# Merge, projection and feed-forward stages share a block; last chunks run tile by tile

## The chip, the cores and the metric

The kernel runs on one core of a Trainium2 chip. The core has a matrix engine (PE), a vector engine (DVE), a scalar engine (ACT), a general engine (POOL) and a queue engine (SP) that only issues DMAs here. The metric is the device time of one execution in microseconds, lower is better.

## What is computed

Two transformer stacks of two layers each, in float32, on 512 tokens with 1024 features. The part of a layer that the change touches reads, for the first stack:

```
x = x + (g_a * o_a + g_b * o_b + g_c * o_c) @ w_out
h = rms_norm(x, g_ffn)
x = x + jnp.square(jax.nn.relu(h @ w_ff1)) @ w_ff2
```

and for the second stack (two branches, six modulation vectors from `c @ mod_w[l] + mod_b[l]`):

```
x = x + g1 * _mixer(h, positions, w_in[l], forget_bias[l], w_branch_a[l], w_branch_b[l], w_out[l])
h = _rmsnorm(x, norm2_g[l]) * (1.0 + sc2) + sh2
x = x + g2 * _conv_ffn(h, w_up[l], conv_w[l], conv_b[l], w_down[l])
...
    u = conv_b + sum(conv_w[i] * up[:, i:i + S] for i in range(CONV_W))
    a, b = jnp.split(u, 2, axis=-1)
    return (jax.nn.silu(a) * b) @ w_down
```

## The kernel before

Activations are kept transposed: a tile is 128 features by 512 tokens, and x has eight (k = 0 to 7). A product runs in split precision: `moving_hi` (a_hi) is the rounded tile and `moving_lo` (a_lo) the rest, and the weights have the same two parts. A chunk is one slab of weights, 128 by 1024, and yields one PSUM bank in most stages: eight tiles k, each three matmuls (high by high, high by low, low by high), 24 matmuls of 128x512. SP loads slabs into a ring of four. For each chunk ACT makes the high weights (L208), POOL subtracts to get the low weights (L234), both into two buffers that alternate. ACT also makes the high part of a tile (L250 or L2295) and DVE the low part (L255 or L2320).

The stages of a layer in question, in order, are:

- `merge_stage`: each branch's output times its projection, gated on DVE (L1178, L1211, L1213) and added to `scratch` (L1188, L1218). 12 chunks of half height in the first stack, 8 in the second; its last chunk fills two banks, output tiles 6 and 7. In the second stack DVE also multiplies modulation weights (L2490), and PE sums them over partitions with one-column matmuls (L2451, `over_partitions`).
- `linear_stage` ("projection", wout): eight chunks, one bank each. DVE adds the bank to x (L2365, or L2909 in the second stack), ACT squares it (L540), DVE adds up the squares (L548).
- First stack, `squared_up_stage` ("up"): 32 chunks. PE sums the squares over partitions (L2276), ACT and DVE make the reciprocal root (L2297 to L2326), PE spreads it (L2281). Each bank is evacuated by DVE with relu and that root (L2331) and squared on ACT (L2307).
- Second stack: a `norm_stage` (not touched), then `gated_up_stage`: 44 chunks, ACT copies each bank (L2828), DVE does the three taps of the convolution and the gate (L2866 to L2879, L2857), ACT the sigmoid (L2821).
- `down_stage`: contracts the hidden tiles, two per block, into all eight banks (L648, at the end L634).

Each stage opens a block of its own. All engines end it together: each drains, they meet at a barrier (L117), POOL clears the semaphores of the block before, and all start the next. Inside a stage, semaphores order the work. A stage's first two chunks are interleaved in `first_products` (L312): for each tile k as soon as it is split, high and low weights of chunk 0 on its high part, then chunk 1, then the low parts. `keep_busy` (L290) issues matmuls on a constant whose result nobody reads, at the ends of stages.

A matmul on full float32 data (one column, 128 columns, or L290's) is one row of the instruction order but two records in the trace.

## Time and profile before

| | us |
|---|---|
| three timed runs | 3581.09, 3584.23, 3584.91; median 3584.23 |
| profiled execution, whole | 3583.43 |
| its span | 3581.7 |
| PE busy in it | 3437.8 (96%) |
| DVE, POOL, ACT busy | 2015.3, 1586.3, 1436.2 |
| mean granted clock of PE | 0.981 of full speed |

In the timeline rows below, the first number is the start of an instruction (or of several merged ones, "x8") in microseconds from the start of the span, the second its duration. Matmuls are pipelined: eight of them in a row last 1.98 us, but the next starts 1.82 us after the first. What stands in brackets is the idle time of the engine before the row and what ended it.

### The profile page before, as it was taken

What the parts mean: (1) busy time and instruction counts of PE and PEld (TensorE: products, weight loads), DVE (VectorE), ACT (ScalarE), POOL (GpSimd) and SP (SyncE); (2) the same over time, 40 slices, a digit from 0 to 9 for tenths busy, and PEclk for the clock granted to TensorE, in tenths of its full rate; (3) what the DMA queues carried; (4) which work ended last, traced back from release to release, by engine and by line L of the source; (5) the groups of instructions that cost most, each with busy time, mean ns of one, the idle gap of its engine ahead of it and who ended that gap; (6) DMA issues with size and microseconds to landing.
All of it is one profiled execution on the core that took longest, in us unless ns stands there. A gap on an engine that the chain in (4) does not pass through costs nothing. (4 is left out here: it accounts for less than half of the span.)

```text
span 3581.7 us, 44753 instructions
## 1 busy us (share of the span) xinstructions
PE 3437.8 (96%) x15838; PEld 2818.8 (79%) x15838; DVE 2015.3 (56%) x3260; ACT 1436.2 (40%) x2516; POOL 1586.3 (44%) x827
## 2 busy tenths in 40 slices
PE   7999999999999999999999999999999999999998
PEld 6877787788888777878887877778877877778877
DVE  5775655112367756641224666658964666658953
ACT  3256743232333567332323446233333446333332
POOL 3346453444444563534443641335543641335543
PEclk9999999999999999999999999999999999999999
DMA  4311123222232111322343221432343221432322
GB/s 165 103 57 37 36 89 106 93 94 95 88 124 97 45 42 46 114 83 94 106 146 108 72 89 60 165 112 103 131 153 107 72 89 56 164 112 104 134 89 94
DMA packets 96746, 346.62 MB, mean 97 GB/s; under 512 B 12624, under 2 KB 13264, under 8 KB 95952
## 3 DMA queue, kind: packets, MB, share of 16 engines
q1 hardware_dynamic: 96592, 344.62, 27.9%
q8 instruction: 91, 1.49, 0.2%
q14 instruction: 63, 0.52, 0.0%
HBM read 338.15 MB, written 6.29 MB: 96 GB/s over the span
## 5 line engine op out<-in xcount | busy, mean ns | idle before, releaser
L234 POOL TENSOR_TENSOR weights_lo<-arena,weights_hi 128x1024 fp32r<-128x1024 f32 x467 | 1189.8, 2548 | 1616.9 <-ACT weights_hi L208 1468.4
L208 ACT ACTIVATE weights_hi<-arena 128x1024 fp32r<-128x1024 f32 x491 | 517.8, 1055 | 622.7 <-PE ps L648 388.1
L302 PE MATMUL ps<-moving_hi,weights_hi 128*128 128x512 f32 x2256 | 568.8, 395 | 11.7 <-ACT weights_hi L208 6.7
L302 PE MATMUL ps<-moving_lo,weights_hi 128*128 128x512 f32 x2256 | 559.5, 390 | 0.0
L302 PE MATMUL ps<-moving_hi,weights_lo 128*128 128x512 f32 x2256 | 557.7, 389 | 0.0
L302 PEld LDWEIGHTS ps<-moving_hi,weights_hi 128*128 128x128 f32 x2256 | 424.1, 189 | 103.3 <-ACT weights_hi L208 7.1
L302 PEld LDWEIGHTS ps<-moving_lo,weights_hi 128*128 128x128 f32 x2256 | 424.1, 189 | 88.3
L302 PEld LDWEIGHTS ps<-moving_hi,weights_lo 128*128 128x128 f32 x2256 | 423.3, 188 | 87.2
L255 DVE TENSOR_TENSOR moving_lo<-arena,moving_hi 128x512 fp32r<-128x512 f32 x196 | 178.0, 959 | 230.9 <-ACT moving_hi L250 230.9
L2331 DVE SCALAR_TENSOR_TENSOR arena<-ps,arena 128x512 f32 x64 | 44.1, 691 | 306.7 <-PE ps L302 292.6
L1015 ACT ACTIVATE arena<-ps,arena 128x512 f32<-128x512 f32 (+1 forms) x320 | 165.9, 525 | 114.8 <-DVE arena L979 114.6
L648 PE MATMUL ps<-moving_hi,weights_hi 128*128 128x512 f32 x800 | 198.1, 390 | 0.0
L648 PE MATMUL ps<-moving_hi,weights_lo 128*128 128x512 f32 x800 | 197.6, 389 | 0.0
L648 PE MATMUL ps<-moving_lo,weights_hi 128*128 128x512 f32 x800 | 197.6, 389 | 0.0
L399 POOL TENSOR_TENSOR weights_lo<-arena,weights_hi 128x512 fp32r<-128x512 f32 x76 | 97.9, 1300 | 197.3 <-ACT weights_hi L208 151.2
L2828 ACT ACTIVATE arena<-ps 128x512 f32<-128x512 f32 x88 | 52.8, 600 | 318.6 <-PE ps L302 302.6
L979 DVE CUSTOM_DVE_ANT_0 ps<-ps,arena 128x512 f32<-128x512 f32 (+1 forms) x320 | 147.1, 519 | 58.8 <-PE ps L927 29.4
L648 PEld LDWEIGHTS ps<-moving_hi,weights_hi 128*128 128x128 f32 x800 | 149.9, 188 | 32.6 <-ACT moving_hi L250 1.6
L648 PEld LDWEIGHTS ps<-moving_hi,weights_lo 128*128 128x128 f32 x800 | 150.2, 188 | 31.2
L648 PEld LDWEIGHTS ps<-moving_lo,weights_hi 128*128 128x128 f32 x800 | 150.2, 188 | 31.1
L948 PE MATMUL ps<-split,split 128*128 128x512 f32 (+3 forms) x640 | 130.1, 333 | 21.8 <-ACT split L1044 19.9
L2876 DVE SCALAR_TENSOR_TENSOR arena<-arena 128x512 f32<-128x512 f32 x88 | 144.5, 1681 | 0.0
(384 smaller groups left out, 5259.6 us busy)
## 6 DMA issues: line engine op xcount, KB each, us to landing
arena<-wstream SPq DMA_DIRECT2D x532, 512.0 KB, 3.3
arena<-modw SPq DMA_DIRECT2D x64, 512.0 KB, 3.7
arena<-modw_first SPq DMA_DIRECT2D x32, 512.0 KB, 4.1
layer_input<-arena SPq DMA_DIRECT2D x2, 2048.0 KB, 6.9
arena<-layer_input SPq DMA_DIRECT2D x2, 2048.0 KB, 8.0
arena<-xT SPq DMA_DIRECT2D x4, 512.0 KB, 5.5
outT<-arena SPq DMA_DIRECT2D x8, 256.0 KB, 2.1
arena<-con SPq DMA_DIRECT2D x1, 1413.5 KB, 9.4
```

The costliest lines, as they stand in the source:

```text
L208: m.nc.scalar.activation(m.w_hi[:, j % 2, :], slab(m, base + at), ACT.Copy).then_inc(hi_ready, 1)
L234: m.nc.gpsimd.tensor_tensor(m.w_lo[:, j % 2, :], slab(m, base + (j if at is None else at)), m.w_hi[:, j % 2, :].bitcast(F32), ALU.subtract)\
L255: return m.nc.vector.tensor_tensor(m.a_lo[:, k, :], tile, m.a_hi[:, k, :].bitcast(F32), ALU.subtract)
L302: mm = m.nc.tensor.matmul(bank, unit_tile(w, k), a[:, k, :], start=(p == 0 and k == 0), stop=(p == 2 and k == KD - 1))
L399: self.m.nc.gpsimd.tensor_tensor(self.m.w_lo[:, j % 2, part], slab(self.m, self.base + j)[:, part], self.m.w_hi[:, j % 2, part].bitcast(F3 ...
L648: mm = nc.tensor.matmul(m.ps[:, 4 * half + n, :], unit_tile(w[:, j % 2, :], 2 * n + k), a[:, 2 * h + k, :], start=(first and p == 0 and k ...
L948: mm = nc.tensor.matmul(m.ps[:, 6, kt * P:T], values(j, b, kt), m.r(part)[:, PT_AT[kt]:PT_AT[kt] + T - kt * P], start=(p == 0 and kt == 0) ...
L979: r = nc.vector.tensor_tensor_reduce(s, s, masks(u // nb, qt), -1.0, HUGE, ALU.add, ALU.min, mx[:, 4 * (u % 2) + qt:4 * (u % 2) + qt + 1])
L1015: a = nc.scalar.activation(prob[:, u % 2, PROB_AT[qt]:PROB_AT[qt] + P * (qt + 1)], m.ps[:, bank, c:c + P * (qt + 1)], ACT.Exp, bias=mx[:, ...
L2331: nc.vector.scalar_tensor_tensor(m.hidden[:, i * BODY + g, :], m.ps[:, g, :], 0.0, rstd, ALU.max, ALU.mult).then_inc(evaced, 1)
L2828: nc.scalar.activation(u[:, s, 2:W], m.ps[:, s, :], ACT.Copy).then_inc(copied, 1)
L2876: nc.vector.scalar_tensor_tensor(acc[:, s, :], u[:, s, 0:T], column(cw, f), acc[:, s, :], ALU.mult, ALU.add).then_inc(tap3, 1)
```

## The change

`chain` opens one block for several stages, and `stage` inside it only adds semaphores. In the first stack merge, projection, up and down of a layer are one chain; in the second stack merge and projection are one, and gated up and down another. A stage now returns an `After`: for the next stage it names the semaphore and count by which a tile of the moving operand has been read (`released`), a tile of the next stage's source is final (`ready`), a bank has been evacuated (`freed`), all weights have been read (`finished`), and functions with the work that the old stage leaves to be put into the next one's program (`act_tail`, `dve_tail`, `pe_tail` and others). The last chunk of a stage runs through `last_products`: for each tile k its three matmuls, then a signal. In merge the last chunk's loops over k and over the three products are swapped. The dummy matmuls between chained stages are dropped. In the second stack the modulation sums of gated up stand before its last four chunks, and those of merge inside the first products of projection. The first turn of the down stage's ACT loop and the last turn of the up stages' loops are written out. `first_layer` wraps merge, `linear_stage(..., leave=True)`, `squared_up_stage` and `down_stage` in one `with chain(m)`.

```diff
@@ -108,21 +109,46 @@
...
 @contextmanager
-def stage(m, names):
-
...
-    ctx = ExitStack()
+def chain(m):
+    ctx, sems = ExitStack(), []
     m.parity = 1 - m.parity
-    sems = [ctx.enter_context(m.nc.semaphore(f"{s}_{m.parity}")) for s in names.split()]
     with m.nc.Block() as block:
...
-        yield block, sems
+        m.chain = block, ctx, sems
+        yield
+    m.chain, m.high_by, m.low_by = None, None, None
     if m.used:
         m.used[0].close()
     m.used = (ctx, sems)
+@contextmanager
+def stage(m, names):
+    with nullcontext() if m.chain else chain(m):
+        block, ctx, sems = m.chain
+        mine = [ctx.enter_context(m.nc.semaphore(f"{s}_{m.parity}_{len(sems)}")) for s in names.split()]
+        sems.extend(mine)
+        yield block, mine
+After = namedtuple("After", "finished released ready freed order total all_ready slots_read act_lead act_tail dve_tail dve_end pe_tail",
...
@@ -303,33 +335,51 @@
...
+    order = after.order or range(KD)
...
+    if after.freed:
+        take(pe, after.freed(0))
+    for n, k in enumerate(order):
+        pe.wait_ge(src_hi, n + 1)
+        product(0, m.w_hi, a_hi, k, start=(n == 0))
...
+    if after.freed:
+        take(pe, after.freed(1))
+    for n, k in enumerate(order):
+        product(1, m.w_hi, a_hi, k, start=(n == 0))
+    if middle:
+        middle(pe)
+    for n, k in enumerate(order):
+        pe.wait_ge(src_lo, n + 1)
+        mm = product(0, m.w_hi, a_lo, k, stop=(n == KD - 1))
     mm.then_inc(chunk_done, 1)
...
+def last_products(pe, m, j, count, bank, hi_ready, lo_ready, released, chunk_done):
+    w_hi, w_lo = m.w_hi[:, j % 2, :], m.w_lo[:, j % 2, :]
+    pe.wait_ge(hi_ready, count)
+    pe.wait_ge(lo_ready, count)
...
+        for p, (w, a) in enumerate(((w_hi, m.a_hi), (w_hi, m.a_lo), (w_lo, m.a_hi))):
+            mm = m.nc.tensor.matmul(bank, unit_tile(w, k), a[:, k, :], start=(k == 0 and p == 0), stop=(k == KD - 1 and p == 2))
+        mm.then_inc(released if k < KD - 1 else chunk_done, 1)
...
@@ -475,104 +525,120 @@
...
+            if leave:
+                if after.freed:
+                    take(pe, after.freed(last))
+                last_products(pe, m, last, body, m.ps[:, last, :], hi_ready, lo_ready, released, chunk_done)
...
+            for k in order:
+                if after.released:
+                    act.wait_ge(*after.released(k))
+                    act.wait_ge(*after.ready(k))
+                split_hi(m, k, source(k)).then_inc(src_hi, 1)
+            for g in range(body):
+                weights_hi(act, m, base, 0, g + 1, body, chunk_done, hi_ready, after=after)
...
+                if g == 0:
+                    act.wait_ge(src_lo, KD)
+                if g < last or not leave:
+                    square(act, g)
...
+            for n in range(2):
+                low(dve, n)
+            if after.dve_tail:
+                after.dve_tail(dve)
+            for n in range(2, KD):
+                low(dve, n)
+            if after.dve_end:
+                after.dve_end(dve)
+            take(dve, after.all_ready)
...
@@ -637,13 +705,13 @@
...
-                    if half == 0 and first and p == 0:
-                        keep_busy(m, 7, 2)
...
                     for n in range(4):
+                        if first and p == 0 and after.freed:
+                            take(pe, after.freed(4 * half + n))
...
@@ -673,19 +741,31 @@
         def _(act):
             def cut(i, h):
                 for k in range(2):
+                    if isinstance(i, int) and i == 0 and after.released:
+                        act.wait_ge(*after.released(2 * h + k))
+                        act.wait_ge(*after.ready(2 * h + k))
                     split_hi(m, 2 * h + k, hidden(i * 4 + 2 * h + k)).then_inc(src_hi, 1)
...
+            if after.act_lead:
+                after.act_lead(act)
+            block_(0, 0, True)
+            block_(0, 1, True)
...
@@ -1099,10 +1182,12 @@
...
-                            for p, (w, a) in enumerate(((m.w_hi, m.a_hi), (m.w_hi, m.a_lo), (m.w_lo, m.a_hi))):
-                                for k in range(4):
+                            for k in range(4):
+                                for p, (w, a) in enumerate(((m.w_hi, m.a_hi), (m.w_hi, m.a_lo), (m.w_lo, m.a_hi))):
                                     mm = nc.tensor.matmul(m.ps[:, 2 * j + n, :], unit_tile(w[:, j % 2, :], 4 * n + k),
                                                           a[:, 4 * (b % 2) + k, :], start=(p == 0 and k == 0), stop=(p == 2 and k == 3))
+                                if n and k < 3:
+                                    mm.then_inc(released, 1)
                             mm.then_inc((first_done, chunk_done)[n], 1)
...
@@ -1132,12 +1217,6 @@
...
-            pe.wait_ge(gated, 8 * (NB - 1) + 2)
-            if not modulate:
-                keep_busy(m, 0, 3)
-            else:
-                pe.wait_ge(mod_added, KD)
-                over_partitions(m, [m.mod_accs[:, q, :] for q in (0, 2)], 0).then_inc(mod_summed, 1)
...
+            last(dve, 6, first_done, 1)
+        def dve_tail(dve):
+            last(dve, 7, chunk_done, 4 * NB + 1)
...
+        def dve_end(dve):
+            dve.wait_ge(mod_summed, 1)
+            for n, part in enumerate((2, 4)):
+                add_modulation_bias(m, part, 1, m.ps[:, 7, KD * n:KD * (n + 1)]).then_inc(mod_biased, 1)
+            dve.wait_ge(mod_biased, 2)
+            modulated_gain(m, 1, 4, "g2")
+        def pe_tail(pe):
+            pe.wait_ge(gated, 8 * NB)
+            pe.wait_ge(mod_added, KD)
+            over_partitions(m, [m.mod_accs[:, q, :] for q in (0, 2)], 7).then_inc(mod_summed, 1)
...
+        return After(finished=(chunk_done, 4 * NB + 1), released=tile_released, ready=lambda k: (added, 8 * (NB - 2) + k + 1),
+                     freed=lambda n: (mod_biased, 2) if modulate and n == 7 else (gated, 8 * (NB - 1) + n + 1),
+                     order=(0, 1, 2, 3, 4, 5, 6, 7) if in_last else (4, 5, 0, 1, 2, 3, 6, 7),
+                     all_ready=(unparked, 16) if parked else None, slots_read=(mod_added, KD) if modulate else None,
+                     dve_tail=dve_tail, dve_end=dve_end if modulate else None, pe_tail=pe_tail if modulate else None)
...
@@ -2263,62 +2364,90 @@
...
-            keep_busy(m, 6, 3)
+            for g in range(BODY - 1):
+                pe.wait_ge(evaced, (iters - 2) * BODY + g + 1)
+                chunk(iters - 1, g)
+            pe.wait_ge(evaced, COUNT - BODY)
+            last_products(pe, m, BODY - 1, COUNT, m.ps[:, BODY - 1, :], hi_ready, lo_ready, released, chunk_done)
...
         def _(act):
+            def high(k):
+                act.wait_ge(*after.released(k))
+                act.wait_ge(*after.ready(k))
+                nc.scalar.activation(m.a_hi[:, k, :], m.x[:, k, :], ACT.Copy, scale=gain(k)).then_inc(src_hi, 1)
             weights_hi(act, m, base, 0, 0, BODY, chunk_done, hi_ready)
-            for k in range(KD):
-                nc.scalar.activation(m.a_hi[:, k, :], m.x[:, k, :], ACT.Copy, scale=gain(k)).then_inc(src_hi, 1)
+            for k in range(KD - 1):
+                high(k)
+            weights_hi(act, m, base, 0, 1, BODY, chunk_done, hi_ready, after=after)
+            after.act_tail(act)
+            high(KD - 1)
             act.wait_ge(summed, 1)
             nc.scalar.activation(root, m.ps[:, SUMS_BANK, 0:TT], ACT.Sqrt, bias=m.eps, scale=1.0 / D).then_inc(rooted, 1)
             nc.scalar.activation(var, m.ps[:, SUMS_BANK, 0:TT], ACT.Identity, bias=m.eps, scale=1.0 / D).then_inc(rooted, 1)
-
...
+            weights_hi(act, m, base, 0, 2, BODY, chunk_done, hi_ready)
+            act.wait_ge(spread_done, 1)
+            nc.scalar.activation(rstd, m.ps[:, SPREAD, :], ACT.Copy).then_inc(spread_out, 1)
...
+            for k in range(KD - 2):
+                low(k)
+            after.dve_tail(dve)
+            low(KD - 2)
+            after.dve_end(dve)
+            low(KD - 1)
...
@@ -2800,13 +2934,27 @@
...
-            with pe.Fori(1, 11) as i:
+            with pe.Fori(1, 10) as i:
...
             pe.wait_ge(mod_added, KD + 1)
             over_partitions(m, [acc_mod], 5).then_inc(mod_summed, 1)
-            keep_busy(m, 6, 4)
+            for s in range(3):
+                pe.wait_ge(copied, 40 + s + 1)
+                split_products(pe, m, base, 10, s, 4, m.ps[:, s, :], hi_ready, lo_ready).then_inc(chunk_done, 1)
+            pe.wait_ge(copied, 44)
+            last_products(pe, m, 3, 44, m.ps[:, 3, :], hi_ready, lo_ready, released, chunk_done)
...
@@ -2925,23 +3088,25 @@
...
+    with chain(m):
+    with chain(m):
+        up = gated_up_stage(m, spare, normed_tiles(m, spare, gain(1), mod(3)))
+        down_stage(m, C2["ff_down"], NF2 // 2, gated_add(5), m.layer + 1 if m.layer + 1 < DEPTH else None, up)
```

How it moves instructions. ACT where projection hands over to up in layer 0 of the first stack; L540 are squares, L208 high weights, L2295 the eight high parts, L2297 and L2298 the root and its argument, L2304 copies the spread root. Before:

```order
L208 ACTIVATE weights_hi<-arena 128x1024
L540 ACTIVATE arena<-arena 128x512
L117 UNCONDITIONAL_BRANCH
L2291 UNCONDITIONAL_BRANCH
L2295 ACTIVATE moving_hi<-arena 128x512 x8
L2297 ACT_TABLE_LOAD
L2297 ACTIVATE arena<-ps,arena 128x4
L2298 ACTIVATE arena<-ps,arena 128x4
L208 ACTIVATE weights_hi<-arena 128x1024
L2304 ACTIVATE arena<-ps 128x512
L2307 ACTIVATE arena<-arena 128x512
L208 ACTIVATE weights_hi<-arena 128x1024
```

After (L238 high weights, L2410 high parts, L570 the square of tile 7, L2419 and L2420 root, L2423 the spread root):

```order
L238 ACTIVATE weights_hi<-arena 128x1024
L2405 UNCONDITIONAL_BRANCH
L2410 ACTIVATE moving_hi<-arena 128x512 x7
L238 ACTIVATE weights_hi<-arena 128x1024
L570 ACTIVATE arena<-arena 128x512
L2410 ACTIVATE moving_hi<-arena 128x512
L2419 ACT_TABLE_LOAD
L2419 ACTIVATE arena<-ps,arena 128x4
L2420 ACTIVATE arena<-ps,arena 128x4
L238 ACTIVATE weights_hi<-arena 128x1024
L2423 ACTIVATE arena<-ps 128x512
L238 ACTIVATE weights_hi<-arena 128x1024
```

The square of tile 7 has moved behind seven high parts and the second chunk's high weights, the eighth high part behind it, and a further chunk's high weights stand before the first square of up.

DVE at the same place; L2365 adds the last bank to x, L548 adds squares, L2320 makes low parts. Before:

```order
L2365 TENSOR_TENSOR arena<-arena,ps 128x512
L548 TENSOR_TENSOR arena<-arena 128x512 x2
L117 UNCONDITIONAL_BRANCH
L2316 UNCONDITIONAL_BRANCH
L2320 SCALAR_TENSOR_TENSOR moving_lo<-arena,moving_hi 128x512 x8
L751 RECIPROCAL arena<-arena 128x4
```

After (L2442 low parts, L2494 the addition to x, L594 the sums of squares):

```order
L2438 UNCONDITIONAL_BRANCH
L2442 SCALAR_TENSOR_TENSOR moving_lo<-arena,moving_hi 128x512 x6
L2494 TENSOR_TENSOR arena<-arena,ps 128x512
L2442 SCALAR_TENSOR_TENSOR moving_lo<-arena,moving_hi 128x512
L594 TENSOR_TENSOR arena<-arena 128x512 x2
L2442 SCALAR_TENSOR_TENSOR moving_lo<-arena,moving_hi 128x512
L835 RECIPROCAL arena<-arena 128x4
```

The evacuation of the last bank has moved behind six low parts.

PE where gated up hands over to down in the second stack; L2451 are the modulation sums, L290 dummies, L648 the first products of down. Before:

```order
L2803 COMPARE_AND_BRANCH
L2451 MATMUL ps<-arena 128x1 x8
L290 MATMUL ps<-arena 128x256 x4
L117 UNCONDITIONAL_BRANCH
L652 UNCONDITIONAL_BRANCH
L290 MATMUL ps<-arena 128x256 x2
L648 MATMUL ps<-moving_hi,weights_hi 128x512 x8
L648 MATMUL ps<-moving_hi,weights_lo 128x512 x8
```

After (L2585 the sums, L334 and L381 gated up's chunks):

```order
L2937 COMPARE_AND_BRANCH
L2585 MATMUL ps<-arena 128x1 x8
L334 MATMUL ps<-moving_hi,weights_hi 128x512 x8
L334 MATMUL ps<-moving_lo,weights_hi 128x512 x8
L334 MATMUL ps<-moving_hi,weights_lo 128x512 x8
...
L381 MATMUL ps<-moving_hi,weights_hi 128x512
L381 MATMUL ps<-moving_lo,weights_hi 128x512
L381 MATMUL ps<-moving_hi,weights_lo 128x512
```

The sums now stand before the last four chunks, the dummies are gone, and the last chunk alternates its three products tile by tile.

## Rows read from the trace of the kernel before

**Rows 1.** The page: busy time by engine; a group with count, busy us, mean ns.

```profile
PE 3437.8 (96%) x15838; PEld 2818.8 (79%) x15838; DVE 2015.3 (56%) x3260; ACT 1436.2 (40%) x2516; POOL 1586.3 (44%) x827
...
L302 PEld LDWEIGHTS ps<-moving_hi,weights_hi 128*128 128x128 f32 x2256 | 424.1, 189 | 103.3 <-ACT weights_hi L208 7.1
```

**Rows 2.** Timeline, handover A: start us, duration, engine, line, operation, [idle before].

```profile
564.44 1.46 PE L290 MATMUL ps<-arena 128*128 128x256 f32 x6
...
579.78 1.98 PE L302 MATMUL ps<-moving_hi,weights_hi 128*128 128x512 f32 x8
```

**Rows 3.** Timeline, handover B, layer 0, PE.

```profile
612.42 1.46 PE L290 MATMUL ps<-arena 128*128 128x256 f32 x6
...
630.22 1.06 PE L2281 MATMUL ps<-arena 128*128 128x128 f32 x8
...
641.80 1.98 PE L302 MATMUL ps<-moving_hi,weights_hi 128*128 128x512 f32 x8
```

**Rows 4.** Timeline, handover C, layer 0, PE.

```profile
797.74 1.98 PE L302 MATMUL ps<-moving_hi,weights_lo 128*128 128x512 f32 x8
...
799.56 1.46 PE L290 MATMUL ps<-arena 128*128 128x256 f32 x6
...
802.90 2.10 PE L648 MATMUL ps<-moving_hi,weights_hi 128*128 128x512 f32 x8
```

**Rows 5.** Timeline, handover D, first layer of the second stack, PE.

```profile
2624.31 1.84 PE L2451 MATMUL ps<-arena 128*128 128x1 f32 x16
...
2626.02 1.97 PE L290 MATMUL ps<-arena 128*128 128x256 f32 x8
...
2632.20 2.12 PE L648 MATMUL ps<-moving_hi,weights_hi 128*128 128x512 f32 x8
```

**Rows 6.** Timeline, handover A2, first layer of the second stack, PE.

```profile
2308.15 1.07 PE L1104 MATMUL ps<-moving_hi,weights_lo 128*128 128x512 f32 x4
...
2330.26 1.98 PE L302 MATMUL ps<-moving_hi,weights_hi 128*128 128x512 f32 x8
```

**Rows 7.** Timeline, handovers A and B of layer 1, PE.

```profile
1529.66 1.46 PE L290 MATMUL ps<-arena 128*128 128x256 f32 x6
...
1545.70 1.98 PE L302 MATMUL ps<-moving_hi,weights_hi 128*128 128x512 f32 x8
...
1578.34 1.46 PE L290 MATMUL ps<-arena 128*128 128x256 f32 x6
...
1609.15 1.98 PE L302 MATMUL ps<-moving_hi,weights_hi 128*128 128x512 f32 x8
```

**Rows 8.** Timeline, last operation of DVE before handover A.

```profile
566.04 0.69 DVE L1218 TENSOR_TENSOR arena<-arena 128x512 f32<-128x512 f32 x1
```

**Rows 9.** Timeline around B: POOL's weights, ACT's high parts, DVE's low parts.

```profile
609.56 2.42 POOL L234 TENSOR_TENSOR weights_lo<-arena,weights_hi 128x1024 fp32r<-128x1024 f32 x1 [3.02 <-ACT weights_hi L208]
...
615.08 5.02 ACT L2295 ACTIVATE moving_hi<-arena 128x512 fp32r<-128x512 f32 x8 [1.11 <-PEq L117]
...
615.84 5.39 DVE L2320 SCALAR_TENSOR_TENSOR moving_lo<-arena,moving_hi 128x512 fp32r<-128x512 f32 x8 [1.13 <-ACT moving_hi L2295]
```

**Rows 10.** Timeline, DVE and POOL at once, after C and at the kernel's start.

```profile
803.88 2.43 POOL L234 TENSOR_TENSOR weights_lo<-arena,weights_hi 128x1024 fp32r<-128x1024 f32 x1 [4.53 <-ACT weights_hi L208]
...
804.35 3.10 DVE L255 TENSOR_TENSOR moving_lo<-arena,moving_hi 128x512 fp32r<-128x512 f32 x2 [0.70 <-ACT moving_hi L250]
...
26.52 4.90 DVE L255 TENSOR_TENSOR moving_lo<-arena,moving_hi 128x512 fp32r<-128x512 f32 x8
...
28.28 5.41 POOL L234 TENSOR_TENSOR weights_lo<-arena,weights_hi 128x1024 fp32r<-128x1024 f32 x1 [3.24 <-ACT weights_hi L208]
```

**Rows 11.** Timeline of narrow matmuls; below, stretch A2 with mean clock after POOL.

```profile
108.30 1.95 PE L1504 MATMUL ps<-arena 128*128 128x1 f32 x16
...
110.11 3.47 PE L302 MATMUL ps<-moving_hi,weights_hi 128*128 128x512 f32 x8
...
2311.00:2323.00 12.00, 10.40 (x41) 8.95 (x41) 6.72 (x14) 5.22 (x9) 1.91 (x1) 0.57 0.36 132
```

455 lines of the change are left out of this document (244 added, 211 removed).

## The prediction

> **What bounds the kernel now.** I read the page's busy line first: PE is busy 3437.8 of 3581.7 us [rows 1]. So only PE's idle time, its dummy matmuls and its slow stretches can be won, and each is looked up in the timeline at the ten places where a stage now hands over inside one block. There I measure from T, the moment at which PE ends the last real chunk of the old stage, to the first row that the change leaves alone. The yardstick is the steady pace: eight 128x512 matmuls in 799.56 - 797.74 = 1.82 us [rows 4], 0.227 us each, so the 48 matmuls of a stage's first two chunks cost 10.9 us and a chunk of 24 costs 5.44.
>
> What each handover takes now:
> - A, merge to projection, first stack: 579.78 - 564.44 = 15.3 us in layer 0 [rows 2] and 1545.70 - 1529.66 = 16.0 in layer 1 [rows 7]; 4.5 and 5.2 above 10.9. The six rows L290 are three dummy matmuls.
> - A2, the same in the second stack: real work ends at 2308.15 + 4 x 0.227 = 2309.06, the third chunk starts at 2330.26 [rows 6]: 21.2 us. Besides 10.9 it holds 32 matmuls with one column (the modulation sums), which stay.
> - B, projection to up: through the end of the third chunk 641.80 - 612.42 = 29.4 us [rows 3], and 1609.15 - 1578.34 = 30.8 in layer 1 [rows 7]. Real work there: 10.9 + 5.44, plus small matmuls: the spread of the root, 1.06 us at L2281 [rows 3], and the sums of squares, taken at the same: 18.4.
> - C, up to down: 802.90 - 799.56 = 3.34 us, all of it dummies and waiting [rows 4]; twice.
> - D, gated up to down: 2632.20 - 2624.31 = 7.89 us [rows 5]; twice.
>
> **The change, part by part.** What goes in all ten is the chain "last bank read, DVE drained, barrier, ACT splits tile 0". What comes instead is a chain by tile: PE releases tile k of the moving operand during its last chunk, ACT writes the new high part, DVE the low part. Since ACT and DVE run in order, I followed their new order by hand with the durations of the old rows. The new order of three matmuls per tile costs PE nothing I can see (the fourth rival has the bound). It asks for the low weights at the chunk's start: POOL has them ready at 609.56 + 2.42 = 611.98 for a chunk that starts at 612.42 [rows 9], so nothing is added.
>
> C. ACT has the first two high parts ready before T. The low parts follow the last evacuation on DVE (0.7 us after T) and are asked for 3.6 us after T. Nothing is late: gain 3.3 us each. The unknown is POOL: its subtraction for the next weights starts about 1.4 us after T and may fall between the two DVE subtractions. Then the second ends about 4.7 us after T, 1.2 late. Bounds 2.1 to 3.3; I take 2.9, nearer the upper since DVE is there first. Sum 5.8.
>
> D. The copy of the last bank (ACT) and the taps (DVE) no longer stand before the first product, which needs only hidden tiles 0 and 1. The 16 one-column matmuls move ahead of the last four chunks and still take 2626.02 - 2624.31 = 1.7 us, so 7.9 - 1.7 = 6.2 is the most. DVE then does the taps of the last pair with POOL's subtractions in between; the low parts of tiles 2 and 3 are due at T + 12.7 and I get them at T + 12.5 where modulations are interleaved. Bounds 4.5 to 6.2; I take 6.2, sum 12.4.
>
> A, first stack. Tile 7 is last. DVE goes: gate and add of tile 6, two low parts, gate and add of tile 7 (0.7 us each, L1218 [rows 8]), and ends some 3.7 us after T, so ACT has tile 7 at T + 4.4 and the second weights at T + 5.5. PE wants tile 7 at T + 3.2 and waits 1.3 us, then 0.6 more for the weights. The six remaining low parts keep ahead of PE. So 10.9 + 1.8 = 12.7 us: gains 2.6 and 3.3. If POOL gets in between, one subtraction is 2.5 us late and about 1 us of it reaches PE: bounds 1.7 to 2.7 and 2.4 to 3.5. Sum 5.9.
>
> A2. The same, but DVE has a modulation product (1.27 us, up to T + 0.7) in front, so tile 7 comes at T + 5.6 and PE idles 2.4 us, then 0.5 for the weights; then the 32 one-column matmuls at 0.107 each (1.71 / 16) take 3.4. That is 10.9 + 2.9 + 3.4 = 17.2 and a gain of 4.0 at full clock. But after 16 one-column matmuls from 108.30 to 110.11, with no idle time, eight wide ones lasted 3.47 us instead of 1.98 [rows 11]: the clock had fallen to its lower level, 1.2 GHz. Here 3.4 us of them come after 2.9 us of idle time, and in the old kernel this very place ran 12 us at a mean clock of 0.57 [rows 11]. I charge 2.5 us: gain 1.5 each, bounds -1.1 (the whole slow stretch remains, 5.1 us) to 4.0. Sum 3.0.
>
> B. The largest term and the least sure. ACT writes seven high parts from T - 3.0 on, 0.63 apart (5.02 / 8), then the second weights (T + 2.4), then the square of tile 7, then high part 7. DVE writes six low parts (0.67 each, 5.39 / 8 [rows 9]) before it evacuates bank 7. The first of them starts under POOL's subtraction and ends only at T + 0.1, so the sixth ends at T + 3.4, the evacuation at T + 4.1, high part 7 at T + 5.4. PE wants it at T + 3.2 and idles 2.2 us. After that nothing is late: sums of squares, low products, and the root's chain (table load, root, five small DVE operations, 2.9 us of it left after the sums) runs under 5.4 us of matmuls. So B takes 18.4 + 2.2 = 20.6 us, 21.5 with half of a slow stretch (3.47 - 1.98 = 1.5 us, about 1.7 where it covers nothing but matmuls) in it; gains 7.9 and 9.3, sum 17.2.
>
> Here a rule matters. The trace shows two behaviours: two DVE subtractions started under POOL's took 3.10 us together [rows 10], and eight back to back held POOL off, whose subtraction took 5.41 instead of 2.43 us [rows 10]. In B POOL wants to subtract at T + 2.5, in the middle of such a run. I go by the second row: POOL waits until the run ends. The Trainium skill, "SBUF — State Buffer", section "Who interferes with whom", says that a DVE instruction with two SBUF inputs and a GpSimd instruction that reads SBUF exclude each other and that the one that issues first holds the shared pair for the whole instruction. By that rule POOL would get in after one DVE instruction. The rows at 26.52 and 28.28 speak against it for a run whose waits are all met. What the other order would give is the second rival.
>
> Sum: 5.9 + 3.0 + 17.2 + 5.8 + 12.4 = 44.3 us. The profiled execution took 3583.43 us (1.7 outside the span), 0.8 less than the median of the three timed runs (3584.23): 3583.4 - 44.3 = 3539.1, and from the median 3539.9. I say 3540.
>
> **The rivals.**
> 1. Everything is covered. Tile 7 arrives in time and the clock never falls: A 6.1, A2 8.0, B 10.3 + 11.7, C 6.7, D 12.4 give 55, time 3529. For it: idle gaps become 2 us or less, and not every such gap lowered the clock (A of layer 0 took 0.7 us less than A of layer 1 [rows 2, 7], with the same gap). Against: tile 7's chain is as long as worked out above.
> 2. DVE and POOL take turns. In B POOL subtracts between two low parts: the sixth is 2.4 us later, the evacuation at T + 6.4, high part 7 at T + 7.6, and PE idles 4.4 us; such a gap is likely to bring a slow stretch, 1.7 to 3.4 us more. B then gains 5.0 + 6.4, C 4.2, A 4.1, A2 2, D 9 to 10: 31 us, time 3553. For it: most single DVE subtractions in the trace that start under POOL's are blocked.
> 3. The handover is not what costs: another wait (the next stage's weights, the ring) ends as late as the barrier did. Then 0 to 7 us, time 3580. Against: at every one of the ten places the low weights are finished before T, by 0.2 to 0.8 us.
> 4. Slower: the tile-by-tile chunk itself. Six whole chunks and the last chunk of four merges, 6 x 24 + 4 x 24 = 240 matmuls, now change the weights tile and the moving tile together and signal after each tile. If each matmul waited for its own weights load (0.19 us, 424.1 / 2256 in the page's group [rows 1]) and for the one before it to end (1.98 - 7 x 0.227 = 0.39 us [rows 4]), it would take 0.58 instead of 0.227: 240 x 0.35 = 85 us, time 3624. It decides from 0.41 us per matmul on (44.3 / 240 + 0.227). Against: the four at L1104 [rows 6] change both tiles with each matmul and end after 1.07 us, 3 x 0.227 + 0.39.
>
> **How the numbers follow.** Forecast (tile 7 paces, the clock falls now and then) 0.57; rival 1 0.13; rival 2 0.24; rival 3 0.03; slower 0.03. The forecast's own range is 3532 to 3548; where slow stretches fall elsewhere in the kernel shifts with the time and adds about 3 us either way. The range 3526 to 3557 takes in rivals 1 and 2 and leaves out about 1 in 7. About 0.2% (7 us) is what a measurement of this kernel can tell from no change: faster 0.94, same 0.03, slower 0.03.
>
> **What would show it.** The L322 dummies are gone at the ten places. C: the first product of down starts where the last up matmul ends. D: no gap, and 16 one-column matmuls before the last four chunks. B: one gap of about 2.2 us before the eighth pair of products and the third chunk ending 21 us after T; a gap near 4.4 is rival 2, none is rival 1. A: gaps of 1.3 and 0.6. A2: the rows with one column take 3.4 us at full clock or more when it fell. The tile-by-tile chunks take 5.4 us. I am wrong if a gap ends on the low weights, or if high part 7 is not what PE waits for in B.

## The result and the profile after

| | before | after |
|---|---|---|
| timed runs, median (us) | 3584.57 (3581.09 to 3586.81, 4 runs) | 3555.90 (3553.42 to 3557.26, 4 runs) |
| ratio, 95% interval | | 0.9922 (0.9909 to 0.9936) |
| profiled execution, span (us) | 3583.43, 3581.7 | 3553.42, 3551.6 |
| PE busy, mean granted clock | 3437.8, 0.981 | 3417.2, 0.984 |

The change wins 28.7 us between the medians and 30.0 between the two profiled executions. The forecast was a gain of 44.3, to 3540 us. For each handover the two traces give the time from T (the end of the old stage's last real chunk) to the first row left alone, as in the prediction. At C, "restart" is what the first matmuls after a wait take over the steady pace.

| handover | before | after | won | forecast |
|---|---|---|---|---|
| A layer 0 / layer 1 | 15.34 / 16.04 | 13.38 / 13.41 | 2.0 / 2.6 | 2.6 / 3.3 |
| B layer 0 / layer 1 | 29.4 / 30.8 | 24.0 / 22.1 | 5.4 / 8.7 | 7.9 / 9.3 |
| C layer 0 / layer 1 | 3.3 + restart 0.1 | 0.71 idle, 0.3 restart | 2.5 / 2.5 | 2.9 / 2.9 |
| A2 first / second layer | 21.2 / 21.2 | 20.5 / 23.7 | 0.7 / -2.6 | 1.5 / 1.5 |
| D first / second layer | 7.9 / 7.9 | 1.7, and 5.8 lost later / 1.7 | 0.4 / 6.2 | 6.2 / 6.2 |
| sum | | | 28.4 | 44.3 |

The other 1.7 us of the span's 30.1 are mostly slow stretches that fell elsewhere in the two executions: between 290 and 315 us the granted clock reads 0.86 before and 1.00 after. Every handover is a stretch of PE's timeline: start, duration, line, operation, count, [idle time before <- what ended it].

B, layer 0 (answers to [rows 3]); L345 are the first products of up.

```profile
607.19 0.39 PE L345 MATMUL ps<-moving_hi,weights_hi 128*128 128x512 f32 x1
...
614.70 0.79 PE L345 MATMUL ps<-moving_hi,weights_hi 128*128 128x512 f32 x1 [4.17 <-ACT moving_hi L2410]
...
631.15 1.98 PE L334 MATMUL ps<-moving_hi,weights_hi 128*128 128x512 f32 x8
```

B, layer 1 (answers to [rows 7]); the same code, another gap:

```profile
1560.92 0.39 PE L345 MATMUL ps<-moving_hi,weights_hi 128*128 128x512 f32 x1
...
1566.27 0.58 PE L345 MATMUL ps<-moving_hi,weights_hi 128*128 128x512 f32 x1 [2.02 <-ACT moving_hi L2410]
...
1583.00 1.98 PE L334 MATMUL ps<-moving_hi,weights_hi 128*128 128x512 f32 x8
```

PE waits for high part 7 in both, as the prediction says. 2.02 us was its forecast (2.2), 4.17 its second rival (4.4). DVE and POOL at the two places, layer 0 first:

```profile
605.19 7.58 DVE L2442 SCALAR_TENSOR_TENSOR moving_lo<-arena,moving_hi 128x512 fp32r<-128x512 f32 x6 [1.95 <-ACT moving_hi L2410]
612.69 0.68 DVE L2494 TENSOR_TENSOR arena<-arena,ps 128x512 f32<-128x512 f32 x1
...
609.86 2.36 POOL L266 TENSOR_TENSOR weights_lo<-arena,weights_hi 128x1024 fp32r<-128x1024 f32 x1 [3.10 <-ACT weights_hi L238]
```

```profile
1558.91 5.43 DVE L2442 SCALAR_TENSOR_TENSOR moving_lo<-arena,moving_hi 128x512 fp32r<-128x512 f32 x6 [1.09 <-ACT moving_hi L2410]
1564.27 0.68 DVE L2494 TENSOR_TENSOR arena<-arena,ps 128x512 f32<-128x512 f32 x1
1564.86 2.25 DVE L2442 SCALAR_TENSOR_TENSOR moving_lo<-arena,moving_hi 128x512 fp32r<-128x512 f32 x1
...
1563.59 2.98 POOL L266 TENSOR_TENSOR weights_lo<-arena,weights_hi 128x1024 fp32r<-128x1024 f32 x1 [3.10 <-ACT weights_hi L238]
```

In layer 0 POOL takes its 2.4 us (2.36) inside the run of six low parts, which lasts 7.58 us; in layer 1 it takes 2.98 from its issue, the six last 5.43, the evacuation (which reads PSUM) follows at once, and the low part behind that is blocked instead (2.25).

D, first layer (answers to [rows 5]): the first product of down (L716) stands right at T, but 23.7 us later, at 2620.87, PE waits 4.07 us, and the eight matmuls behind last 3.56 instead of 1.98.

```profile
2597.14 1.98 PE L716 MATMUL ps<-moving_hi,weights_hi 128*128 128x512 f32 x8
...
2624.94 3.56 PE L716 MATMUL ps<-moving_lo,weights_hi 128*128 128x512 f32 x8 [4.07 <-DVE moving_lo L287]
```

SP's first load there, and DVE from the second pair of low parts (the row of 2607.33) to the third, for which PE waits; L2578 is a modulation product, and two that aren't shown stand between:

```profile
2606.51 0.33 SPq L666 DMA_DIRECT2D arena<-modw_first  x1
...
2607.33 1.66 DVE L287 TENSOR_TENSOR moving_lo<-arena,moving_hi 128x512 fp32r<-128x512 f32 x2
2609.69 3.26 DVE L2578 SCALAR_TENSOR_TENSOR arena<-arena 128x1024 f32<-128x1024 f32 x1 [0.70 <-DMA arena<-modw_first]
...
2620.72 2.96 DVE L2578 SCALAR_TENSOR_TENSOR arena<-arena 128x1024 f32<-128x1024 f32 x1 [2.36 <-DMA arena<-modw_first]
2623.60 1.28 DVE L287 TENSOR_TENSOR moving_lo<-arena,moving_hi 128x512 fp32r<-128x512 f32 x2
```

A2, both layers (answers to [rows 6]): gap, eight wide matmuls, 32 one-column sums (L2585), the low parts; then a stretch of each (the second layer first) with the granted clock third from the end.

```profile
2280.34 0.39 PE L345 MATMUL ps<-moving_hi,weights_hi 128*128 128x512 f32 x1
...
2285.70 0.50 PE L345 MATMUL ps<-moving_hi,weights_hi 128*128 128x512 f32 x1 [1.79 <-ACT moving_hi L282]
...
2286.66 3.68 PE L345 MATMUL ps<-moving_hi,weights_hi 128*128 128x512 f32 x8 [0.21 <-ACT weights_hi L238]
2290.16 3.72 PE L2585 MATMUL ps<-arena 128*128 128x1 f32 x32
2293.74 5.45 PE L345 MATMUL ps<-moving_lo,weights_hi 128*128 128x512 f32 x16
...
2300.84 1.98 PE L334 MATMUL ps<-moving_hi,weights_hi 128*128 128x512 f32 x8
...
3088.43 0.39 PE L345 MATMUL ps<-moving_hi,weights_hi 128*128 128x512 f32 x1
...
3097.53 6.82 PE L2585 MATMUL ps<-arena 128*128 128x1 f32 x32
3104.21 6.30 PE L345 MATMUL ps<-moving_lo,weights_hi 128*128 128x512 f32 x16
...
3112.16 1.98 PE L334 MATMUL ps<-moving_hi,weights_hi 128*128 128x512 f32 x8
```

```profile
3096.00:3108.00 12.00, 12.00 (x46) 10.84 (x45) 3.26 (x5) 0.00 (x0) 1.71 (x1) 0.50 0.14 44
...
2285.00:2299.00 14.00, 13.08 (x58) 10.86 (x59) 7.57 (x11) 2.37 (x4) 2.92 (x1) 0.76 0.20 76
```

C (answers to [rows 4]; the first product stands at 788.91, right at T) and A, layer 0 (answers to [rows 2]):

```profile
793.41 2.11 PE L716 MATMUL ps<-moving_lo,weights_hi 128*128 128x512 f32 x8 [0.71 <-DVE moving_lo L287]
```

```profile
561.17 0.39 PE L345 MATMUL ps<-moving_hi,weights_hi 128*128 128x512 f32 x1
...
565.46 0.50 PE L345 MATMUL ps<-moving_hi,weights_hi 128*128 128x512 f32 x1 [0.64 <-ACT moving_hi L282]
...
566.41 2.11 PE L345 MATMUL ps<-moving_hi,weights_hi 128*128 128x512 f32 x8 [0.21 <-ACT weights_hi L238]
568.36 4.54 PE L345 MATMUL ps<-moving_lo,weights_hi 128*128 128x512 f32 x16
...
564.60 5.93 DVE L287 TENSOR_TENSOR moving_lo<-arena,moving_hi 128x512 fp32r<-128x512 f32 x6
...
566.43 2.94 POOL L266 TENSOR_TENSOR weights_lo<-arena,weights_hi 128x1024 fp32r<-128x1024 f32 x1 [6.88 <-ACT weights_hi L238]
```

POOL subtracts inside this run of low parts too: one of the six takes 2.92 us instead of 0.68, and the eighth low part ends at 564.60 + 5.93 = 570.53, T + 9.4.

The last chunk itself, tile by tile, starts at 555.73 in A and ends where L345 starts, 561.17: 5.44 us, the steady pace to the hundredth.

### The profile page after: what moved, and what is told of

It reads as the page before. It is cut to its first block and busy times, and to the rows that moved or that the text cites. A ratio compares the mean times of both kernels' runs of the same rounds, so it can differ in the third digit from the quotient of the medians.

```text
span 3551.6 us, 44405 instructions
## 1 busy us (share of the span) xinstructions
PE 3417.2 (96%) x15770; PEld 2801.4 (79%) x15770; DVE 2033.7 (57%) x3260; ACT 1438.7 (41%) x2516; POOL 1586.2 (45%) x827
## 5 line engine op out<-in xcount | busy, mean ns | idle before, releaser
L238 ACT ACTIVATE weights_hi<-arena 128x1024 fp32r<-128x1024 f32 x491 | 518.0, 1055 | 630.0 <-PE ps L716 383.1
L334 PE MATMUL ps<-moving_hi,weights_hi 128*128 128x512 f32 x2208 | 553.3, 393 | 5.1 <-ACTq L231 5.1
L334 PE MATMUL ps<-moving_lo,weights_hi 128*128 128x512 f32 x2208 | 548.1, 390 | 0.0
L334 PE MATMUL ps<-moving_hi,weights_lo 128*128 128x512 f32 x2208 | 545.9, 389 | 0.0
L334 PEld LDWEIGHTS ps<-moving_hi,weights_hi 128*128 128x128 f32 x2208 | 412.5, 188 | 93.5 <-ACTq L231 6.6
L334 PEld LDWEIGHTS ps<-moving_lo,weights_hi 128*128 128x128 f32 x2208 | 415.2, 189 | 86.3
L334 PEld LDWEIGHTS ps<-moving_hi,weights_lo 128*128 128x128 f32 x2208 | 414.3, 188 | 85.4
L287 DVE TENSOR_TENSOR moving_lo<-arena,moving_hi 128x512 fp32r<-128x512 f32 x196 | 189.6, 1017 | 213.3 <-ACT moving_hi L282 213.3
L716 PE MATMUL ps<-moving_lo,weights_hi 128*128 128x512 f32 x800 | 199.4, 392 | 5.5 <-DVE moving_lo L287 5.5
L716 PE MATMUL ps<-moving_hi,weights_lo 128*128 128x512 f32 x800 | 197.6, 389 | 0.0
L716 PE MATMUL ps<-moving_hi,weights_hi 128*128 128x512 f32 x800 | 197.6, 389 | 0.0
L716 PEld LDWEIGHTS ps<-moving_lo,weights_hi 128*128 128x128 f32 x800 | 151.0, 189 | 38.1 <-DVE moving_lo L287 6.8
L716 PEld LDWEIGHTS ps<-moving_hi,weights_lo 128*128 128x128 f32 x800 | 150.2, 188 | 31.3
L716 PEld LDWEIGHTS ps<-moving_hi,weights_hi 128*128 128x128 f32 x800 | 150.1, 188 | 31.2
L1032 PE MATMUL ps<-split,split 128*128 128x512 f32 (+3 forms) x640 | 130.0, 333 | 21.5 <-ACT split L1128 19.6
```

Of the source, the lines that this page charges most:

```text
L238: m.nc.scalar.activation(m.w_hi[:, j % 2, :], slab(m, base + at), ACT.Copy).then_inc(hi_ready, 1)
L287: return m.nc.vector.tensor_tensor(m.a_lo[:, k, :], tile, m.a_hi[:, k, :].bitcast(F32), ALU.subtract)
L334: mm = m.nc.tensor.matmul(bank, unit_tile(w, k), a[:, k, :], start=(p == 0 and k == 0), stop=(p == 2 and k == KD - 1))
L716: mm = nc.tensor.matmul(m.ps[:, 4 * half + n, :], unit_tile(w[:, j % 2, :], 2 * n + k), a[:, 2 * h + k, :], start=(first and p == 0 and k ...
L1032: mm = nc.tensor.matmul(m.ps[:, 6, kt * P:T], values(j, b, kt), m.r(part)[:, PT_AT[kt]:PT_AT[kt] + T - kt * P], start=(p == 0 and kt == 0) ...
```

## The experiments

Each kernel is the changed one with one edit, unless said otherwise. The same matmuls run in all of them, so each place is compared by the time between the same two matmuls there and in the kernel before (us, minus is faster; for D with what follows it in down). Bold is what the edit aims at. Most kernels ran once, and the kernel before itself took 3575.2 to 3588.9 us over all its runs of this record, so the whole time of a single run tells little and the places carry the argument.

| | A | B | C | A2 | D |
|---|---|---|---|---|---|
| changed kernel | -2.0, -2.6 | -5.4, -8.7 | -2.5, -2.5 | -0.7, +2.6 | -0.4, -6.2 |
| d_low | -1.9, -2.6 | -7.3, -8.7 | -2.5, -2.5 | -0.7, -0.7 | **-6.2**, -6.2 |
| d_sp | -2.0, -2.6 | -4.5, -8.7 | -2.5, -2.5 | -0.7, -0.7 | **-0.1**, -6.2 |
| a2_after | -1.9, -2.6 | -4.4, -5.9 | -2.5, -2.5 | **+3.4, +1.8** | -0.4, -6.2 |
| a2_fill | **-2.0, -2.7** | **-5.1, -8.1** | -2.5, -2.5 | **-3.9, -2.3** | -1.2, -6.2 |
| ca | **-2.0, -2.6** | -8.8, -8.8 | **-3.3, -3.4** | **-3.5, -3.5** | -0.3, -6.2 |
| mix_first | -2.0, -2.7 | -7.3, -5.9 | -2.5, -2.5 | **-3.4, -1.8** | -0.4, -6.2 |
| b_dve | -1.9, -2.6 | **-9.8, -11.3** | -2.5, -2.5 | -0.7, -0.6 | -0.6, -6.2 |
| b_both | -1.9, -2.6 | **-10.0, -11.4** | -2.4, -2.5 | -2.3, +2.6 | -0.6, -6.2 |
| hold_only | -1.9, -2.7 | **-7.3, -8.7** | -2.5, -2.5 | -0.7, +0.5 | -0.4, -6.2 |
| b_hold | -2.0, -2.7 | **-10.1, -11.5** | -2.5, -2.5 | -0.7, -0.6 | -0.5, -6.2 |
| passes | **-2.0, -2.6** | **-7.3, -8.8** | **-2.5, -2.5** | **-0.7, +2.6** | **-0.4, -6.2** |
| all2 | **-2.0, -2.6** | **-9.9, -11.3** | **-3.3, -3.4** | **-3.5, -3.4** | **-6.2**, -6.2 |

The unbold entries are repeats without an edit: A, C and the second D come back within 0.1 us. B's gap takes one of two values, and with the slow stretch behind it, which comes or not, B lies between -4.4 and -8.8 in layer 0 and between -5.9 and -8.8 in layer 1. A2 stands at -0.7 in most kernels, at up to +2.6 in the second layer, and the first D between -0.1 and -1.2.

**Is it the tile by tile chunk?** In `last_products` and in merge's last chunk:

```diff
-    for k in range(KD):
-        for p, (w, a) in enumerate(...):
+    for p, (w, a) in enumerate(...):
+        for k in range(KD):
             mm = ...
-        mm.then_inc(released if k < KD - 1 else chunk_done, 1)
+            if p == 2:
+                mm.then_inc(released if k < KD - 1 else chunk_done, 1)
```

> One of the two parts of the change undone: the stages stay chained, but the last chunk runs its three products in passes over all tiles again, and each tile is released in the last pass, so from T - 1.6 on instead of from T - 4.8 on. Theory: at B and C the pace is set by the low parts, the last bank and the order of ACT and DVE, not by the first releases, and PE uses 0.454 us per tile while ACT makes one in 0.63; so each of the ten places differs from the changed kernel by less than 1 us (B may still take either of its two values, 2 us apart), and the sum of A, C and D by less than 1.5 us. Rival: the tile by tile order carries the gain; then every place loses up to 3.2 us, A, B and C most, 20 us or more in all.

Measured: no place is slower; time 3549.8 in one run. The gap in B is 1.56 us in both layers, and layer 0 of B is even 1.9 us faster than in the changed kernel. So the shared block carries the gain, and releasing tiles earlier than T - 1.6 brings nothing.

```profile
613.37 0.61 PE L345 MATMUL ps<-moving_hi,weights_hi 128*128 128x512 f32 x1 [1.56 <-ACT moving_hi L2411]
```

**D: what stands before the low parts.**

```diff
                 modulations(0, 0)
+                cut(1, 0)
                 modulations(0, 1)
...
-                    for h in range(2):
-                        cut(i, h)
-                        modulations(i, h)
+                    cut(i, 1)
+                    modulations(i, 0)
+                    cut(i + 1, 0)
+                    modulations(i, 1)
```

> Beside the changed kernel only one thing moves: in the down stages with modulation products DVE makes the low parts of the next pair of hidden tiles one half turn earlier, ahead of two of the four products that stood before them. Theory: the 4.07 us gap of PE at 2620.87 in the changed kernel (and the slow stretch behind it, 3.56 for 1.98 us, 1.6 us) comes from low parts queued behind four products whose loads SP may not start before the last hidden tile is done. Then gap and stretch go, the first down stage of the second stack ends 5 to 6 us earlier, the whole near 3550. Rival: the DVE instruction blocked by POOL (2.96 us for a product of 1.28) sets it; then a gap of 2 us or more stays, 2 us are won at most. Second rival: the products end later and the end of the stage waits for them; then the gap shows up in front of its last modulation sums and nothing is won.

Measured: the gap is gone, 5.8 us won in D, time 3543.4 in one run (B and A2 came out better too, without an edit there). DVE still waits for loads and is still blocked by POOL (3.17 us for a product), but the low parts stand after two products, and PE has them some 2.5 us before it needs them:

```profile
2610.17 3.17 DVE L2586 SCALAR_TENSOR_TENSOR arena<-arena 128x1024 f32<-128x1024 f32 x1 [0.81 <-DMA arena<-modw_first]
...
2615.09 3.52 DVE L287 TENSOR_TENSOR moving_lo<-arena,moving_hi 128x512 fp32r<-128x512 f32 x2
```

That the loads start late was to be shown by starting them earlier:

```diff
                 cut(0, 0)
+                for q in range(2):
+                    nc.vector.memset(m.mod_accs[:, q, :], 0.0).then_inc(mod_added, 1)
                 if after.dve_tail:
                     after.dve_tail(dve)
-                for q in range(2):
-                    nc.vector.memset(...)
...
-                     all_ready=(pair_done, 22), ...
+                     all_ready=(tap3, 48), ...
```

> Beside the changed kernel: SP begins the loads of down behind the third tap of the last pair (all that reads the place the slots take) and not behind the last hidden tile, and the two clears of the accumulators stand ahead of the last taps. Loads start near T + 5, not T + 9.4; the first product starts about 4 us earlier; the low parts of the third pair, 0.3 us ahead of where PE wants them. Theory (loads late): gap of 4.07 us falls below 1 us, 4 to 5.7 us won. Rival (the four products before the low parts, or POOL's block, whatever the loads): gap stays above 3 us, within 1 us of no change.

Measured: D -0.1, the gap 3.89 us, so by its numbers the rival's side. But the edit did not do what it was to do: the clears delay the taps, and SP's first load stands at T + 8.0 (2607.41 - 2599.40) instead of T + 9.4. The first modulation product starts at T + 13.0 (2612.37) instead of T + 12.5, not 4 us earlier. The run says nothing for the late loads or against them.

```profile
2607.41 0.33 SPq L666 DMA_DIRECT2D arena<-modw_first  x1
```

**B: why two values.** Over the changed kernel and the five runs with B unchanged (d_low, d_sp, a2_after, ca, mix_first) the gap was 2.02 or 2.03 us seven times and 4.17 to 4.23 five times. To take the choice away, POOL waits ahead of up's second low weights (`behind` is `(src_lo, KD)`):

```diff
         for j in range(body):
+            if j == 1:
+                take(pool, behind)
             weights_lo(pool, m, base, 0, j, body, hi_ready, lo_ready)
```

> Beside the changed kernel one wait is added: at handover B POOL does not start the low weights of up's second chunk before DVE has made all eight low parts. Among the changed kernel and the five runs of it with B unchanged, PE's gap ahead of the last pair was 2.02 us seven times and 4.2 us five times. Theory: the value is decided by whether POOL's subtraction, which becomes free 0.02 us before DVE's sixth low part, goes first and blocks it (2.89 us for a low part of 0.74) or goes behind. Held back, POOL cannot: the gap is 2.0 us in both layers, B at -7.3 to -7.6 in layer 0 and -8.7 to -9 in layer 1. PE wants the low weights some 10 us behind T and gets them at T + 10, so up to 0.5 us may be lost there. Rival: the value comes from something else (an ACT instruction, the clock); then 4.2 us still shows in one of the two places with even chances, or a value of its own.

Measured: 2.02 us in both layers, and no low part is blocked behind the first. B is -7.3 and -8.7, no better than without the hold where the gap was 2.02. So POOL's subtraction is what makes 4.2 out of 2.0. Which of the two goes first is close to the order in which they become free: in the six kernels above and a2_fill POOL's record starts ahead of that of DVE's sixth low part in all 14 places, by 18 to 32 ns where POOL went first (7) and by 15 to 20 ns where DVE did (7).

```profile
613.71 0.63 PE L347 MATMUL ps<-moving_hi,weights_hi 128*128 128x512 f32 x1 [2.02 <-ACT moving_hi L2412]
```

**B: DVE's and ACT's order.** On DVE, then on ACT:

```diff
-            for k in range(KD - 2):
-                low(k)
-            after.dve_tail(dve)
-            low(KD - 2)
-            after.dve_end(dve)
-            low(KD - 1)
+            low(0)
+            after.dve_tail(dve)
+            for k in range(1, 4):
+                low(k)
+            after.dve_end(dve)
+            for k in range(4, KD):
+                low(k)
```

> Beside the changed kernel only DVE's order at handover B moves: one low part, then the evacuation of bank 7, then three low parts, the two additions of squares, and the last four low parts. Places are compared by the time between the same two matmuls in this kernel and in the kernel before; the changed kernel's B stands at -5.4 and -8.7 us. Theory: PE's idle time ahead of the last pair (4.17 and 2.02 us) is the evacuation queued behind six low parts, one of them blocked by POOL or not. Now bank 7 is evacuated by T + 0.9, and what is left is ACT's order: second weights, square, high part 7 at T + 3.8, so PE idles 0.6 to 0.8 us. B stands at -9.5 in layer 0 and -11 in layer 1, with no difference of 2 us between the layers any more. Rival: POOL's subtraction (free from T + 2.6 on) blocks an addition of squares by 2.4 us; then the wait moves ahead of the sums of squares, about 1 us, and may take either value by layer. Rival two: the gap does not come from DVE's order; then it stays at 2 to 4 us.

Measured: -9.8 and -11.3, 0.3 better than the theory, gaps 0.46 and 0.28 us in both layers. The block of the first rival came too: of the two additions of squares one met POOL's subtraction (the two take 3.70 us, 1.48 else), which leaves the gap of 0.28.

```profile
612.58 0.50 PE L345 MATMUL ps<-moving_hi,weights_hi 128*128 128x512 f32 x1 [0.46 <-ACT moving_hi L2410]
...
615.42 1.02 PE L2379 MATMUL ps<-arena 128*128 128x1 f32 x8 [0.28 <-DVE arena L594]
```

```diff
-            for k in range(KD - 1):
+            for k in range(KD):
                 high(k)
             weights_hi(act, m, base, 0, 1, ...)
             after.act_tail(act)
-            high(KD - 1)
```

> As the run with DVE's new order at handover B, and also on ACT: high part 7 stands ahead of the second weights and the square of tile 7. High part 7 is made by T + 2.3, PE wants it at T + 3.2; the second weights end at T + 3.3, PE wants them at T + 3.6. Theory: no idle time of PE at B before the sums of squares; B at -10.3 in layer 0 and -11.7 in layer 1, that is 0.7 us better than with DVE's order alone. Rival: the square of tile 7 comes 0.7 us later than before and the sums wait for it, so that nothing or 0.5 us is lost instead.

Measured: -10.0 and -11.4. The first gap is gone and the second grew to 0.87. An addition of squares still meets POOL's subtraction (2.55 us for 0.69), and it is now the second one, which starts later since it waits for ACT's square: of 0.7 us expected 0.15 came.

```profile
614.12 1.02 PE L2379 MATMUL ps<-arena 128*128 128x1 f32 x8 [0.87 <-DVE arena L594]
...
611.42 2.55 DVE L594 TENSOR_TENSOR arena<-arena 128x512 f32<-128x512 f32 x1 [0.30 <-ACT arena L570]
```

With POOL held as above:

> As the run with both orders changed at B (DVE and ACT), whose one gap was 0.87 us ahead of the sums of squares, behind an addition of squares of 0.69 us that took 2.55 beside POOL's subtraction; and POOL is held back until the eight low parts are made. Theory: the addition takes 0.7 us, the gap of 0.87 goes, B at -10.8 in layer 0 and -12.3 in layer 1 (they stood at -10.0 and -11.4). Rival: POOL's low weights for the second chunk are then late by 0.5 us or more and the gap stands ahead of its last pass; B within 0.3 us of the run without the hold.

Measured: the addition takes 0.69 and that gap is gone, but B is -10.1 and -11.5 all the same. POOL now does two subtractions in one go, and two tiny operations of the root's chain (128x4, 0.17 us else) take 2.40 and 2.35 beside them; the spread of the root is 0.84 late. The block moved on to the next instructions with two SBUF inputs.

```profile
615.20 2.40 DVE L839 TENSOR_TENSOR arena<-arena 128x4 f32<-128x4 f32 x1
...
615.16 4.80 POOL L266 TENSOR_TENSOR weights_lo<-arena,weights_hi 128x1024 fp32r<-128x1024 f32 x2 [7.61 <-DVE moving_lo L2443]
...
620.76 1.16 PE L2388 MATMUL ps<-arena 128*128 128x128 f32 x8 [0.84 <-DVE arena L2457]
```

**A2: what lowers the clock.** First the sums behind the first products instead of in their middle:

```diff
-... src_lo, chunk_done, after, after.pe_tail)
+... src_lo, chunk_done, after)
+            if after.pe_tail:
+                after.pe_tail(pe)
```

> Beside the changed kernel: the 32 one-column modulation sums of merge stand behind the first two chunks of the projection, not in their middle. In the changed kernel handover A2 takes 20.5 us in the first layer and 23.7 in the second, with the clock at 0.5 for 3.4 us behind the 1.8 us gap and again through and behind the sums. Theory idle: the gap ahead of tile 7 is what lowers the clock; only the first slow stretch (1.7 us) stays and the second layer wins about 5 us, the first about 1.7. Rival narrow: the sums lower it; the stretch goes with them, the third chunk takes 7 us or more instead of 5.44, and nothing is won over both layers within 1.5 us.

Measured: 4.1 us slower in the first layer, and in the second 0.8 faster than in the changed kernel but 2.5 slower than the -0.7 of other kernels. The edit brought a wait of its own, 2.95 us of PE behind the sums, since DVE adds the biases ahead of the first evacuation and ACT makes the next weights behind that; the slow stretch behind the sums can be the wait's as well. What it does show: with no sums between them, the low parts of both layers ran at a clock of 1.00 once the gap's stretch was over (4.33 and 4.56 us, against 5.45 and 6.30 in the changed kernel). Next four dummies in the gap:

```diff
     for n, k in enumerate(order):
+        if n == KD - 1 and after.freed:
+            take(pe, after.freed(2))
+            keep_busy(m, 2, 4)
         pe.wait_ge(src_hi, n + 1)
```

> Beside the changed kernel: ahead of the pair of products of the last tile PE issues four dummy matmuls (128x256, about 1.9 us) at handovers A, A2 and B. Theory idle (the gap lowers the clock): no slow stretch behind the filled gap, A2 takes 18 to 19 us in both layers, B loses its 1.4 to 1.7 us of slow clock; A in the first stack becomes 1.2 us longer, since its gap was only 0.6. Rival narrow: the stretch behind the gap goes but the one behind the sums stays, A2 20 us or more. Rival neither: all stretches stay where they were.

Measured: A2 -3.9 and -2.3; the clock stays at 1.00 in the first layer and is lowered once, behind the sums, in the second. The expected 18 to 19 us became 17.3 and 18.9. At B the dummies end before the wait does, and 2.5 us of idle time stay. POOL went first in both layers there, as in a2_after (-4.4, -5.9); beside that kernel B is 0.7 and 2.2 us better, and in layer 1 no slow stretch followed. A is not 1.2 us longer, as was expected, since there the low parts pace PE. Mean clock in 12 us of the two layers:

```profile
2290.00:2302.00 12.00, 11.84 (x68) 10.38 (x69) 6.68 (x10) 1.68 (x3) 4.67 (x2) 1.00 0.26 98
3094.00:3106.00 12.00, 11.78 (x62) 10.08 (x61) 6.41 (x9) 1.96 (x3) 2.94 (x1) 0.86 0.16 58
```

Then the gap made short (`after.dve_tail(dve)` ahead of all low parts in `linear_stage`), with the edit for C in the same kernel (the last evacuation of up goes into a `dve_tail`, behind down's first two low parts):

> Two edits at different places. C: the last evacuation of up moves behind the two first low parts of down on DVE (they only need high parts made 1.5 us ahead of T). In the changed kernel PE idles 0.71 us there and C stands at -2.5 in both layers; theory (second pair of low parts, one of them blocked by POOL, is late): gap gone, C at -3.3. Rival: the evacuation is then blocked and the square and high part of the last tile come later; same gap a few us further on. A and A2: DVE gates and adds tile 7 ahead of the two low parts that stood between tile 6 and tile 7, 1.3 us earlier. A stands at -2.0 and -2.6, A2 at -0.7 and +2.6: theory (tile 7 paces): PE's gap of 0.64 us goes and A gains 0.8 more; in A2 the gap of 1.79 falls to 0.5, with it the slow stretch behind it (1.7), so A2 stands at -3.5 to -4 in both layers if no stretch follows the sums, at -2 if one does. Rival: the low parts, 1.3 us later, become late themselves and give it back.

Measured: C -3.3 and -3.4, as expected. A2 -3.5 in both layers, gap 0.59 and no slow stretch behind it, one behind the sums. A wins nothing, against 0.8 expected: its gap is gone, but the low parts start later, eight in 7.13 us with POOL's subtraction among them, and the eighth ends at 573.58, T + 9.4 as in the changed kernel. PE waits for them.

```profile
566.45 7.13 DVE L287 TENSOR_TENSOR moving_lo<-arena,moving_hi 128x512 fp32r<-128x512 f32 x8
...
568.63 2.59 POOL L266 TENSOR_TENSOR weights_lo<-arena,weights_hi 128x1024 fp32r<-128x1024 f32 x1 [6.03 <-ACT weights_hi L238]
...
571.83 4.14 PE L345 MATMUL ps<-moving_lo,weights_hi 128*128 128x512 f32 x12 [0.17 <-DVE moving_lo L287]
```

Last, with that edit, the sums spread over the low products:

> A and A2 as in the run before (tile 7 ahead of the low parts), and in A2 the 32 one-column records do not stand in one row of 3.4 us but four behind each of the eight wide products of the low parts of the first chunk. Theory narrow: a row of one-column matmuls with no wide ones in it is what brings the second slow stretch; mixed, no stretch follows, A2 at -4 or better in both layers. [...] Rival two: changing between the two kinds costs PE time; the eight pairs then take over 5.6 us at full clock.

Measured: -3.4 and -1.8, no better. The clock falls during or behind the spread sums too (0.50 from 3100 to 3104). So the idle gap brings one slow stretch: with it made short or filled, none came in eight places. A second one comes during or behind the 32 narrow matmuls, mixed or not; that they cause it is likely but not shown, since no run leaves them out.

**Together.** The edits of d_low, ca and b_dve, and on ACT high part 7, then the square, then the second weights:

> All edits that won something, together: in down the low parts ahead of the second half of the modulation products; at A and A2 tile 7 ahead of the low parts; at B DVE's order low part, evacuation, three low parts, squares, four low parts, and on ACT high part 7, then the square of tile 7, then the second weights; at C the last evacuation behind the first two low parts. The places do not touch each other, so their differences to the kernel before should add up: A -2.0 and -2.6, B -10.5 and -11.9 (0.5 us each better than with the second weights ahead of the square, since the squares are then added before POOL's subtraction starts), C -3.3 twice, A2 -3.5 twice, D -6.2 twice: 53 us, and 1 to 3 us either way from slow stretches elsewhere. Time 3528 to 3534, ratio to the kernel before 0.984 to 0.986. Rival: an earlier start at one place brings a later wait or slow stretch elsewhere; then the places add up but the span does not follow, 3540 or more.

Measured: 3535.13 us (3531.73 to 3537.18, 4 runs), ratio to the kernel before 0.9867 (0.9851 to 0.9884), about 21 us below the changed kernel; its interval does not touch that one's. The median lies 1 us above the 3528 to 3534 that were expected. The ten places give 51.9 of the 53 expected, and the span follows them (51.8), so the rival is out. B lacks 0.6 in each layer: the squares are added before POOL starts, but POOL then blocks the low parts behind (four in 4.90 us).

```profile
611.71 4.90 DVE L2451 SCALAR_TENSOR_TENSOR moving_lo<-arena,moving_hi 128x512 fp32r<-128x512 f32 x4
```

## Why the prediction was right, and where it was wrong

The direction and the range held (3526 to 3557, measured 3555.9), and nine of the ten places gained (A2 in the second layer lost), but the time lies at the range's edge, outside the forecast's own 3532 to 3548, and the gain is two thirds of the forecast. It is nearest to rival 2's 3553, and that is partly luck: POOL's turns account for about 4.6 of the 15.9 us that are missing (B in layer 0, A and C), while 10.7 are a queue at D that nobody followed and the clock at A2. By its steps:

- **Yardsticks and C, D second layer.** 5.44 us for a tile by tile chunk held: rival 4 is out. D of the second layer won 6.2, as worked out. C won 2.5 for 2.9: PE waits 0.71 us for the second pair of low parts, which POOL's subtraction blocks as feared (four low parts take 4.72 us there), and the value lay nearer the lower of its bounds.
- **D, first layer (5.8 too much), the step that failed.** I followed the low parts to the second pair, due at T + 12.7; they were done at 2607.33 + 1.66, T + 11.9. The third pair I did not follow. It stands behind four modulation products, and these behind loads that SP may start only when the last hidden tile is done: at T + 9.4, while in the old block it was 2 us after down's start (2634.22 - 2632.20). So the pair was done 27.7 us after down's start and PE wanted it at 23.7, a wait that the sum put at nothing; behind it came 1.6 us of slow clock. In the old kernel it was done at 18.3 (2649.24 + 1.28 - 2632.20), with 5 us of room; chaining took that. In d_low the third pair's place alone cured it. The share of the late loads and of POOL's blocks (3.26 and 2.96 us for products of 1.28) isn't settled, since d_sp moved the loads by 1.4 us only.
- **B (3.1 too much).** The working was right for one layer: gap 2.02 for 2.2, though the whole slow stretch came (22.1 us for 21.5). In the other layer rival 2 came. I had made one choice for both; it is near a tie within one kernel, and hold_only shows that POOL's turn is what decides. I had read the rows at 26.52 and 28.28 [rows 10] as "POOL waits until the run ends". In five of twelve cases POOL entered the run; in the other seven the run ended with the very instruction it had to let pass, so they don't speak for my reading. At A and A2 POOL entered the run of low parts in both layers of all thirteen kernels, 52 of 52 (in ca with 2.59 us in the middle of eight). The rule of the Trainium skill, "SBUF — State Buffer", section "Who interferes with whom", that the one that issues first holds the pair for one whole instruction, agrees with these in that no block is longer than one instruction. It does not settle the near ties (at two places POOL's record starts 18 ns ahead, and it went first at one only), and the 5.41 us at 28.28 remain unexplained by it: there five low parts, each with its own record, went ahead of POOL.
- **A (1.3 too much).** The wait for tile 7 and the weights was sized well: 565.46 - 561.17 - 14 x 0.227 = 1.1, and 0.5 for the weights, against 1.3 and 0.6. The step "the six remaining low parts keep ahead of PE" was wrong: the sixteen matmuls that need them take 572.74 - 568.36 = 4.4 us instead of 3.63. The cause is the case that the prediction named for its bounds and left out of its value: POOL got in between, one low part was 2.2 us late (2.92 for 0.68), and 0.8 us of that reached PE. ca shows that the low parts are the bound, since it takes the gap away and wins nothing.
- **A2 (4.9 too much).** Waits of 2.7 us for 2.9 and sums of 3.6 for 3.4 were right; the mis-sized term is the clock. I charged 2.5 us and it was 3.4 in the first layer (two stretches at the lower level, 1.2 GHz: 1.7 in the eight matmuls at 2286.66, 1.7 in the low parts) and 6.7 in the second, where the clock was at 0.50 from 3096 to 3108, through the sums and into the low parts. The lower bound of -1.1 was passed (-2.6).

Rivals 1 and 3 are out: gaps are there, and no place kept its barrier's time. Two numbers of these rivals were wrong, without weight for the forecast. With everything covered and the clock never falling, the prediction's own yardsticks give A 4.4 + 5.2, A2 2 x 6.9, B 11.0 + 12.4, C 6.7 and D 12.4, 66 us and not 55, so rival 1 would have been 3518 us, below the stated range. And the low weights are finished 0.2 to 0.8 us before T at six of the ten places; at A and A2 it is 1.6 us.

## What to carry to other kernels

When a barrier goes, follow each in-order queue (SP's too) past the handover until the stages run steadily again: the cost of D came back 24 us later, in DVE's queue, whose order had not changed but whose room had. Put what the next engine waits for ahead of what it needs later, one low part, then the evacuation, and count the whole row of DVE instructions behind it, since a gap that moves to the low parts wins nothing. Two instructions that exclude each other and become free within 0.02 us are a tie: forecast both.

## What the runs showed of the hardware

- At the handovers a run of DVE instructions with their waits met does not hold POOL off. POOL gets in behind one of them, and the next that has two inputs in SBUF pays, however small it is: a low part at A took 2.92 us instead of 0.68, one at B 2.89 instead of 0.74, and an operation on 128x4 took 2.40 instead of 0.17. Evacuations from PSUM beside POOL kept their 0.68. One place goes the other way: at the kernel's start POOL's subtraction takes 5.41 us (5.42 in the changed kernel), behind five low parts.
- At A2 the eight wide matmuls behind the idle gap of 1.8 us ran slowly (2.75 to 3.52 us up to the next matmul, 1.94 to 1.97 elsewhere) in 13 of the 18 places that had it over these runs, and in none of the 8 where the gap was 0.6 or filled with dummies. During or behind the 32 one-column matmuls the clock fell in 7 of those 8 as well. Yet at D, where 16 of them (1.7 us) now stand between full chunks with no idle time, the eight wide ones behind took 1.9 us up to the next in all 26 places, with no slow stretch, while the prediction had read 3.47 us behind 16 of them at 110.11. What else decides it isn't settled: the same code gave A2 of the second layer -0.7 in four kernels, +0.5 in one and +2.6 in two, and passes, which differs only in the last chunk, +2.6.

```profile
2573.58 1.84 PE L2585 MATMUL ps<-arena 128*128 128x1 f32 x16
2575.28 2.07 PE L334 MATMUL ps<-moving_hi,weights_hi 128*128 128x512 f32 x8
```
